# A hybrid decoder trunk: the channel sums of the convolution's layer norm move from TensorE to GpSimd, with a new order of the convolution stage

## What is computed

```python
def conv_module(xn, w_pw1, b_pw1, w_dw, b_dw, ln_g, ln_b, w_pw2, b_pw2):
    u = xn @ w_pw1 + b_pw1
    a, g = jnp.split(u, 2, axis=-1)
    u = a * jax.nn.sigmoid(g)
    u = lax.conv_general_dilated(
        u, w_dw[:, None, :].astype(u.dtype), window_strides=(1,),
        padding=[(CONV_WIDTH - 1, 0)], dimension_numbers=("NWC", "WIO", "NWC"),
        feature_group_count=u.shape[-1]) + b_dw
    u = jax.nn.silu(layer_norm(u, ln_g, ln_b))
    return u @ w_pw2 + b_pw2

h = x
for i in range(DEPTH):
    xn = rms_norm(h, g_mix[i])
    # i == 0: h = h + conv_module(...);  i == 1: h = h + nsa_attention(...)
    ...
    h = h + hier_moe(rms_norm(h, g_ffn[i]), ...)
    gate = jax.nn.sigmoid(rms_norm(h, g_ple[i]) @ ple_w_gate[i])
    h = h + gate * (p[i] @ ple_w_proj[i])
```

## Time and profile before

| | us |
|---|---|
| median of 3 runs | 1394.39 |
| lowest and highest | 1392.05 and 1396.95 |
| the profiled execution | 1397.69 |
| its span in the profile | 1395.9 |

### The profile page before, as it was taken

How to read it: one execution, slowest core, us unless ns; L and a number is a source line. 1 busy time by engine, 2 the same in 40 slices (tenths; PEclk the granted TensorE clock), 3 DMA queues, 4 the chain that set the end, 5 groups by cost and what they waited for, 6 DMA issues and landing times.

```text
span 1395.9 us, 27964 instructions
## 1 busy us (share of the span) xinstructions
PE 1070.2 (77%) x10442; PEld 602.4 (43%) x10443; DVE 310.5 (22%) x931; ACT 286.6 (21%) x664; POOL 424.4 (30%) x731
## 2 busy tenths in 40 slices
PE   6898977767767667768999889686677677676768
PEld 5673544433434334334455555343333333343433
DVE  4794310000000000004136671200000000000011
ACT  3453311111111111112112571111111111111111
POOL 2100064343343343340000130453433433452520
PEclk9998999887888888889999699898988888888979
DMA  9913379999999999994315502799999999997940
GB/s 309 389 35 132 121 304 429 428 428 429 428 428 428 428 429 428 428 424 160 127 60 211 212 30 106 317 377 428 429 428 429 429 430 428 428 428 322 430 193 31
DMA packets 62733, 448.79 MB, mean 322 GB/s; under 512 B 10826, under 2 KB 21698, under 8 KB 38114
## 3 DMA queue, kind: packets, MB, share of 16 engines
q1 hardware_dynamic: 57634, 447.73, 77.4%
q10 hardware_dynamic: 5056, 0.48, 0.3%
HBM read 447.14 MB, written 1.05 MB: 321 GB/s over the span
## 4 chain that ended last, share of the span: by engine, by line
DMA 45%; PE 42%; DVE 5%; issue 4%; ACT 2%; SPq 1%; ACTq 0%; POOL 0%; DVEq 0%
DMA ring<-in_moe_w_up 43%; PE PS L557 14%; PE PS L436 9%; PE PS L509 2%; PE PS L536 2%; DMA ring<-in_moe_w_down 2%; PE PS L572 2%; PE PS L544 1%; PE PS L763 1%; PE PS L736 1%; PE PS L579 1%; DMA ppw<-in_conv_w_dw 1%; SPq L316 1%; PE PS L819 1%; PE PS L424 1%
## 5 line engine op out<-in xcount | busy, mean ns | idle before, releaser
L557 PE MATMUL PS<-ring,arena 128*32 128x256 f32 x4128 | 342.4, 495 | 212.8 <-DMA ring<-in_moe_w_up 189.3
L557 PEld LDWEIGHTS PS<-ring,arena 128*32 128x32 f32 x4128 | 161.3, 137 | 383.3 <-issue 233.5
L1451 DVE TENSOR_TENSOR arena<-PS,arena 64x256 f32<-64x256 f32 x65 | 27.8, 428 | 637.2 <-ACT arena L1176 630.9
L572 PE MATMUL PS<-ring,arena 128*32 128x256 f32 x2080 | 125.7, 381 | 30.8 <-DVE arena L1454 30.8
L1176 ACT ACTIVATE arena<-PS 64x256 f32<-64x256 f32 x64 | 24.2, 378 | 551.1 <-PE PS L557 551.1
L977 POOL TENSOR_SCALAR arena<-arena 128x32 f32<-128x32 f32 x64 | 18.9, 295 | 342.3 <-PE PS L544 339.4
L936 POOL TENSOR_SCALAR arena<-arena 128x512 f32<-128x512 f32 x67 | 105.7, 1578 | 24.1 <-POOL arena L983 12.9
L572 PEld LDWEIGHTS PS<-ring,arena 128*32 128x32 f32 x2080 | 73.1, 109 | 61.1 <-issue 37.4
L930 POOL TENSOR_SCALAR arena<-arena 128x32 f32<-128x32 f32 x260 | 88.7, 364 | 13.1 <-POOL arena L977 12.9
L938 POOL TENSOR_TENSOR arena<-arena 128x512 f32<-128x512 f32 x67 | 85.4, 1274 | 5.6
L544 PE MATMUL PS<-hn,arena 128*32 128x256 f32 x1072 | 76.7, 401 | 9.3 <-DMA ring<-in_moe_w_down 8.9
(11 more groups left out here) (316 smaller groups left out, 1211.0 us busy)
## 6 DMA issues: line engine op xcount, KB each, us to landing
ring<-in_moe_w_up SPq DMA_DIRECT2D x64, 2048.0 KB, 22.9
ring<-in_moe_w_down SPq DMA_DIRECT2D x64, 2048.0 KB, 24.6
ring<-in_moe_w_gate SPq DMA_DIRECT2D x63, 2048.0 KB, 18.6
wb<-in_ple_w_gate SPq DMA_DIRECT2D x4, 2048.0 KB, 19.0
ring<-in_conv_w_pw SPq DMA_DIRECT2D x3, 2048.0 KB, 18.3
ring<-in_nsa_w_in SPq DMA_DIRECT2D x3, 2048.0 KB, 19.8
wb<-in_nsa_w_in SPq DMA_DIRECT2D x2, 2048.0 KB, 10.8
wb<-in_nsa_cmp_w SPq DMA_DIRECT2D x2, 2048.0 KB, 8.1
```

Source lines behind the costliest of these rows:

```text
L557: i = pe.matmul(PS[32 * j:32 * j + 32, BGU, 0:256].rearrange("q (p c) -> q p c", c=2), xT[:, k, :], w[:, k, :].rearrange("q (p h c) -> q h ...
L572: i = pe.matmul(PS[32 * j:32 * j + 32, BY, 0:Q4], hT[:, c, 32 * f:32 * f + 32], w_dn(s)[:, f, c, Q4 * j:Q4 * (j + 1)], start=(q == 0), sto ...
```

## The change

- TensorE's order becomes pw1(c), taps(c-2), and channel_sums is gone. VectorE adds the tap sum of chunk c-2 in its step c, one later than before. The pivot comes one chunk later, so chunk 2 gets it by an extra add at c = 4.
- GpSimd adds chunks 1 to 5 and their squares to lsum (layer_sums, two adds of 128x256 each); TensorE sums lsum and the chunks 6 and 7 at the end.
- The pw2 bias is loaded to all partitions (into wb's second buffer) and GpSimd adds it to the residual h in two adds of 128x1024 behind its diagonals of chunk 6. The eight one-row matmul records before taps(7) are gone. The load of the second ple_w_gate half waits for these adds, on SyncE's queue.
- The tap transposes come after pw1(0); VectorE copies wdw out after glu(0); wst is now copied from wdw by ScalarE, 16 copies between sigmoid(0) and its first stack copies.
- The small loads: the router group of layer 0 at c = 5, the router group of layer 1 and the positions behind the silus.
- mu and var use the two sigmoid buffers. VectorE's moe waits for GpSimd's bias adds.

```diff
@@ sync @@
             expert(0, 0, 0)
             sp.wait_ge(pw1_mm, 4)
-            for n in range(2):
-                sp.dma_start(dense(WB[n]), cols(ple_w_gate[0], n)).then_inc(ple_in[n], 16)
+            sp.dma_start(bpw2, conv_b_pw2.broadcast_to([P, D])).then_inc(x_in, 16)
+            sp.dma_start(dense(WB[0]), cols(ple_w_gate[0], 0)).then_inc(ple_in[0], 16)
+            sp.wait_ge(hb_ok, 2)
+            sp.dma_start(dense(WB[1]), cols(ple_w_gate[0], 1)).then_inc(ple_in[1], 16)
             sp.wait_ge(pw1_mm, 8)
-            sp.dma_start(bpw2, conv_b_pw2).then_inc(w2_in[0], 16)
             gate_up_load(0, 1, R1[0], 0, gu_in[1])
@@ tensor: taps, and the chunk loop @@
-                pe.wait_ge(xst_act, c + 1)
+                pe.wait_ge(xst_act, c + 2)
                 pe.wait_ge(xst_dve, c + 1)
...
                 i.then_inc(pw1_mm, 1)
-                if c == 2:
+                if c == 0:
+                    tap_columns()
+                if c == 3:
                     pivot_sum()
-                if c >= 1:
-                    taps(c - 1)
-                if c >= 3:
-                    channel_sums(c - 3)
-            channel_sums(KD - 3)
-            pe.wait_ge(w2_in[0], 32)
-            for n in range(2):
-                for t in range(NT):
-                    pe.matmul(PS[:, 2 * n + t, :], ones[0:1, :], bpw2[:, 512 * n:512 * (n + 1)], start=True, stop=False)
-            taps(KD - 1)
+                if c >= 2:
+                    taps(c - 2)
             for c in range(KD - 2, KD):
-                channel_sums(c)
-            pe.wait_ge(w2_in[1], 16)
+                taps(c)
+            pe.wait_ge(ln_acc, 2 * (KD - 3))
+            pe.matmul(PS[:, 6, 0:T], ones[:, :], lsum[:, 0, :], start=True, stop=False)
+            pe.matmul(PS[:, 7, 0:T], ones[:, :], lsum[:, 1, :], start=True, stop=False)
+            for c in range(KD - 2, KD):
+                pe.wait_ge(conv_ok, c + 1)
+                i = pe.matmul(PS[:, 6, 0:T], ones[:, :], cT[:, c, :], start=False, stop=(c == KD - 1))
+            i.then_inc(lnmm, 1)
+            for c in range(KD - 2, KD):
+                pe.wait_ge(ln_sq, c + 1)
+                i = pe.matmul(PS[:, 7, 0:T], ones[:, :], sqb[c % 2], start=False, stop=(c == KD - 1))
+            i.then_inc(lnmm, 1)
@@ gpsimd @@
+            def layer_sums(c):
+                if c < 3:
+                    pool.wait_ge(ln_c, c + 1)
+                else:
+                    pool.wait_ge(conv_ok, c + 1)
+                pool.wait_ge(ln_acc, 2 * (c - 1))
+                g.tensor_tensor(lsum[:, 0, :], cT[:, 0, :] if c == 1 else lsum[:, 0, :], cT[:, c, :], ALU.add).then_inc(ln_acc, 1)
+                pool.wait_ge(ln_sq, c + 1)
+                g.tensor_tensor(lsum[:, 1, :], sqb[0] if c == 1 else lsum[:, 1, :], sqb[c % 2], ALU.add).then_inc(ln_acc, 1)
+
             for c in range(KD):
                 if c >= 2:
                     pool.wait_ge(tap_mm, c - 1)
...
+                if c >= 4:
+                    layer_sums(c - 3)
+                if c == 6:
+                    pool.wait_ge(x_in, 16 * (NT + 1))
+                    pool.wait_ge(hn_dve, 1)
+                    pool.wait_ge(hn_act, 1)
+                    for t in range(NT):
+                        g.tensor_tensor(h[:, t, :], h[:, t, :], bpw2, ALU.add).then_inc(hb_ok, 1)
+            layer_sums(KD - 3)
@@ scalar @@
+                if c == 0:
+                    act.wait_ge(vec_ok, 2)
+                    for j in range(STACK):
+                        for q in range(4):
+                            i = nc.scalar.copy(wst[32 * j:32 * j + 32, q, :, :],
+                                               wdw[32 * q:32 * q + 32, :, DVE_TAPS + j::STACK])
+                    i.then_inc(xst_act, 1)
+                if c >= 3:
+                    squares(c - 3)
...
                 i.then_inc(xst_act, 1)
-                if c >= 2:
-                    squares(c - 2)
-                small_loads(c)
-            for c in range(KD - 2, KD):
+                if c == 5:
+                    router_loads(0)
+            for c in range(KD - 3, KD):
                 squares(c)
...
+            router_loads(1)
+            position_loads()
@@ vector @@
             for c in range(KD):
                 glu(c)
                 dve.wait_ge(glu_ok, c + 1)
+                if c == 0:
+                    tap_columns()
+                    dve.wait_ge(tr_ok, 4)
                 stack_copies(c)
-                if c >= 1:
-                    taps_out(c - 1)
-                if c == 0:
-                    dve.wait_ge(tr_ok, 4)
-                if c == 2:
+                if c >= 2:
+                    taps_out(c - 2)
+                if c == 4:
+                    dve.wait_ge(conv_ok, 3)
+                    v.tensor_tensor(cT[:, 2, :], cT[:, 2, :], npv, ALU.add).then_inc(ln_c, 1)
+                if c == 3:
                     dve.wait_ge(conv_ok, 2)
                     dve.wait_ge(lnmm, 1)
```

More of the change, by code:

```diff
@@ L51 @@
 XW = T + STACK * (RUNS - 1)
-N_VEC, N_MISC, N_ATT = 7, 8 + 6, 8
+N_VEC, N_MISC, N_ATT = 7, 1 + 8 + 6, 8
 SCALE = DH ** -0.5
@@ L198, in build @@
         prow = carve(512)
-        mu, var = prow[:, 0:256], prow[:, 256:512]
+        lsum = prow.rearrange("p (a t) -> p a t", a=2)
+        mu, var = sgm
         wdw = carve(8 * TAPS).rearrange("p (c w) -> p c w", c=8)
@@ L206, in build @@
         sqb = [carve(256) for _ in range(2)]
-        bpw2 = xnT[0:1, 4:8, :].rearrange("p k q -> p (k q)")
+        bpw2 = wb[:, 1, 0:D]
         wdw_rows = ppw[0:TAPS, 3072:4096]
@@ L463, in _, with tap_columns @@
             norm_T(0, 1)
-            pe.wait_ge(wdw_in, 16)
-            for c in range(KD):
-                i = pe.transpose(PS[:, 2, c * TAPS:(c + 1) * TAPS], wdw_rows[:, c * P:(c + 1) * P],
-                                 ident[0:TAPS, 0:TAPS])
-            i.then_inc(vtr, 1)
+            def tap_columns():
+                pe.wait_ge(wdw_in, 16)
+                for c in range(KD):
+                    i = pe.transpose(PS[:, 2, c * TAPS:(c + 1) * TAPS], wdw_rows[:, c * P:(c + 1) * P],
+                                     ident[0:TAPS, 0:TAPS])
+                i.then_inc(vtr, 1)
             def taps(c):
@@ L484, in pivot_sum @@
                 pe.matmul(PS[:, 6, T:2 * T], ones[:, :], cT[:, 0, :], start=True, stop=True).then_inc(lnmm, 1)
-            def channel_sums(c):
-                if c < 2:
-                    pe.wait_ge(ln_c, c + 1)
-                else:
-                    pe.wait_ge(conv_ok, c + 1)
-                i = pe.matmul(PS[:, 6, 0:T], ones[:, :], cT[:, c, :], start=(c == 0), stop=(c == KD - 1))
-                if c == KD - 1:
-                    i.then_inc(lnmm, 1)
-                pe.wait_ge(ln_sq, c + 1)
-                i = pe.matmul(PS[:, 7, 0:T], ones[:, :], sqb[c % 2], start=(c == 0), stop=(c == KD - 1))
-                i.then_inc(lnmm, 1)
             for c in range(KD):
@@ L502, in _ @@
                     pe.wait_ge(glu_ok, c - 3)
-                elif c >= 1:
-                    pe.wait_ge(vec_ok, 3)
+                elif c == 2:
+                    pe.wait_ge(vec_ok, 2)
                 for g in range(2):
@@ L536, in _ @@
                         i = pe.matmul(PS[:, 2 * n + t, :], xnT[:, k, t * P:(t + 1) * P], dense(PW2[n])[:, k, :],
-                                      start=False, stop=(k == KD - 1))
+                                      start=(k == 0), stop=(k == KD - 1))
                     i.then_inc(out_mm, 1)
@@ L758, in _ @@
             for s in range(2):
[L759 removed]
+                pe.wait_ge(w2_in[s], 32)
                 pe.wait_ge(B_ok, s + 1)
@@ L1339, in norm, with tap_columns @@
                     xnT_copy(a, row, t)
-            def first_columns():
+            def tap_columns():
                 dve.wait_ge(vtr, 2)
-                taps = PS[:, 2, 0:8 * TAPS].rearrange("p (c w) -> p c w", c=8)
-                link(v.tensor_copy(wdw, taps))
-                for j in range(STACK):
-                    for q in range(4):
-                        i = v.tensor_copy(wst[32 * j:32 * j + 32, q, :, :],
-                                          taps[32 * q:32 * q + 32, :, DVE_TAPS + j::STACK])
-                i.then_inc(vec_ok, 2)
-                dve.wait_ge(vec_ok, 3)
-                link(v.memset(cv0[:, :, 0:TAPS - 1], 0.0))
+                v.tensor_copy(wdw, PS[:, 2, 0:8 * TAPS].rearrange("p (c w) -> p c w", c=8)).then_inc(vec_ok, 1)
+                dve.wait_ge(vec_ok, 2)
             dve.wait_ge(x_in, 16 * NT)
             norm(0, ROW_MIX)
-            first_columns()
+            link(v.memset(cv0[:, :, 0:TAPS - 1], 0.0))
             def glu(c):
@@ L1396, in _ @@
                         i = v.tensor_scalar(o, u, wdw[:, c, w:w + 1], vecT[:, ROW_BDW + c:ROW_BDW + c + 1], ALU.mult, ALU.add)
-                    elif w == 1 and c < 2:
+                    elif w == 1 and c < 3:
                         i = v.tensor_scalar(o, u, wdw[:, c, w:w + 1], None, ALU.mult)
```

(11 more changed lines are left out.)

46 lines of the change are left out of this document (23 added, 23 removed).

## The result

| us | before | after |
|---|---|---|
| median of 6 runs each | 1395.67 | 1380.81 |
| lowest and highest | 1388.97 and 1400.63 | 1378.07 and 1384.35 |
| span of the profiled execution | 1395.9 | 1379.3 |

The ratio is 0.9884, with a 95% interval of 0.9859 to 0.9909: faster by 1.2%, some 15 us where 5 were forecast. Two repeats, on two chips, gave 0.9900 (0.9869 to 0.9931) and 0.9896 (0.9867 to 0.9924). The sign and the range held; the size did not. The band that the prediction thought likeliest, 1385 to 1392, was missed in all three. The range held only because it took in the time of rival B, and B's mechanism is not what happened, so that part was luck.

What follows compares the result with a forecast made beforehand. The front is bound by engines, chiefly VectorE's convolution chunks, then transfers bind the expert loops. 18.3 + 0.1 - 0.45 - 1.1 - 8.3 - 2.0 - 1.6 = 4.95 us gained, so 1394.4 - 5.0 = 1389.4 us; range 1379 to 1397.

Steps and rivals of the forecast that it cites:

- rival B: Convolution stage: GpSimd waits for gaps between VectorE's instructions, port costs 0 to 3 us, time 1381 to 1384; chance 0.24.
- What bounds the kernel: Front before the expert loads: what the convolution stage gives up moves the third expert's load and the end one for one.
- Idle time, 18.3 us: VectorE's waits before glus 3, 4, 7 and the last tap sum (6.94, 2.06, 0.41, 8.88 us) can be won.
- The start, 0.1 us: Up to glu(1): earlier pw1(0) against ScalarE's wst copies, gain about 0.1 us, bounds -1 to +1.5.
- GpSimd against VectorE, 8.3 + 1.1 us: Convolution chunks: GpSimd's new sums and bias adds block VectorE for 8.3 us (bounds 0 to 9.2), its diagonals 1.1 more.
- the signs to look for: VectorE's timeline: taps of 0.9 us and more under GpSimd's sums, and one of over 2 us at each bias add.
- Router loads, 2.0 us: Chunk 5: the first moved group holds ScalarE before sigmoid(6), making the glu late by 2.0 us, bounds 0 to 10.5.
- Tail and clock, 1.6 us: Stage end: TensorE's low clock costs 0.8 us in pw2, 0.4 on two sums, 0.4 on the last taps.
- Rival D: Pw2's first token half stays at 1.2 GHz, taking 28.1 us instead of 15.67; time 1401.0; chance 0.07.
- E: Convolution stage: VectorE still waits for glus because ScalarE is late; gain about 0, time 1394; chance 0.09.
- C: Before glu(6): ScalarE's queue held as in the first group, 10.5 us idle instead of 2; 1397.9 us; chance 0.10.
- The sum at the last tap sum: End of the convolution stage: the last tap sum would stand near 112.5 us instead of 118.6.

Runs made afterwards that it cites:

- with the loads back: The changed kernel with the small router and position loads at their old places (chunks 2, 3 and 4); 1392.9 us, ratio to before 0.9975.
- with both steps: The changed kernel with GpSimd's bias adds moved ahead of all taps and the channel sums returned to TensorE; 1378.0 us, ratio to before 0.9875.
- the kernel with the early bias: The changed kernel with the bias row loaded early and added by GpSimd ahead of all taps; 1381.1 us, ratio to before 0.9882.
- with the sums on TensorE: The changed kernel with channel sums back on TensorE, one chunk later than before, without GpSimd's ten adds; 1378.6 us, ratio to before 0.9871.

## Why the prediction was right or wrong, step by step

**What bounds the kernel: right.** The third expert's load followed the front (8.6 us earlier for 10.2 us at pw2), and the later loads by 9.8 and 9.9 us. This also held in each experiment: with the loads back, 181.0 for a last tap sum of 118.58; with both steps, 166.0 for 100.13. It is one for one from pw2 on: from there to that load it took 56.5 to 58.8 us in all twelve profiles. Between the last tap sum and pw2 a part can be lost, 5.6 us in before and 7.2 with both steps.

**Idle time, 18.3 us: right.** All of it went, but for 0.46 us in another place.

**The start, 0.1 us: mis-sized.** In the pair glu(1) moved from 35.56 to 34.09, 1.5 us, the upper bound; the other profiles of before and after (34.41 against 33.61 and 32.48) give 0.8 to 1.9. I had allowed 3.4 us for ScalarE's 16 copies and they took 4.12; but pw1(0) began right behind the first transposes:

```profile
15.16 7.51 PE L500 MATMUL PS<-xnT,wb 128*128 128x256 f32 x32
```

It took 7.51 us, while before it began at 16.98 and its gate half was ready for the sigmoid only at 26.81. So glu(0) came at 23.29 instead of 27.40, 4.1 us earlier where 2 were reckoned with; most of it is then lost to ScalarE's copies. In this profile even the first transposes of TensorE started 1.5 us later than in that of before (11.52 and 10.04). In before only 3 or 4 matmuls of pw1(0) start in each microsecond from 17 to 22, where 6 or 7 do from 22 on, and no wait for a load is recorded. They came behind an idle stretch of 2.33 us ahead of the transposes, which the new order has not. In the profile with only the loads moved the same slow stretch stands behind 1.88 us of idle time, and there the granted clock is 0.50 from 18 to 21 us. In before's own profile the clock column says 1.00, so that the clock was the cause there too is likely and not shown.

**GpSimd against VectorE, 8.3 + 1.1 us: right in the main, and by the mechanism.** Adding up what each held row of VectorE took beyond its usual time, all collisions together cost 7.95 us more than before (9.4 predicted): some 4.1 for the ten sums (5.0), 4.3 for the bias adds with the diagonal behind them (4.2). The 1.1 us more for the diagonals did not come: those that are not in the 4.3 cost 3.0 us, and in before all of them had cost 3.4. The prediction had read two of those of before as nearly whole and took two others as smaller; but the copies at 82.50 and 91.86 took 1.97 and 2.01 us too, so most of this price was already paid in before. GpSimd's rows and VectorE's:

```profile
66.60 1.24 POOL L1010 TENSOR_TENSOR arena<-stk,arena 128x512 f32<-128x512 f32 x1 [2.78 <-PE PS L481]
67.81 0.91 POOL L1002 TENSOR_TENSOR arena<-arena,hn 128x256 f32<-128x256 f32 x1
...
83.34 4.88 POOL L1019 TENSOR_TENSOR h<-h,wb 128x1024 f32<-128x1024 f32 x2
```

```profile
66.46 0.48 DVE L1425 SCALAR_TENSOR_TENSOR hn<-ppw,arena,hn 128x256 f32<-128x256 f32 x1
66.85 1.27 DVE L1425 SCALAR_TENSOR_TENSOR arena<-ppw,arena 128x256 f32<-128x256 f32 x1
68.05 0.94 DVE L1425 SCALAR_TENSOR_TENSOR hn<-ppw,arena,hn 128x256 f32<-128x256 f32 x1
```

The question that the trace of before left open is answered: a tap that starts while GpSimd works is held, 1.27 and 0.94 us instead of 0.48. The bias add took 2.44 us (4.88 for two); 2.36 had been extrapolated. Taking the sums and the bias adds away gave 7.2 us back. The bias adds fell on copies and not on taps, as the signs to look for had said, at about the same price; with the loads back they did fall on two taps, which took 2.58 and 2.56 us. Rival B is therefore wrong, though the time that it named, 1381 to 1384, is nearly the one measured: it would have had all taps at 0.48 us.

**Router loads, 2.0 us: the step that failed.** It was priced by the 4.25 us row of before, taken as the one nearest to empty queues. That row lay at 67.91, while weights were still under way; later on the same issue takes 0.46 us. The third issue of a group behind its two loads of short pieces took 12.16 and 15.22 us beside the weights, 4.25 us as they ran out, and 0.45, 0.46 and 0.46 us at 70.39, 77.76 and 78.60, when they were in. So none of the groups issued after the weights were in was held. It is not their end that frees a held issue, as the experiment with the loads back shows, and what does stays open. The weights were not in near 60 us, as had been estimated: in before they run until about 70 us, in after until about 66. The conclusion that no weights would be under way at chunk 5 was right all the same, and the estimate still took a price above nothing, so it gave back 2.0 us that were never paid.

**Tail and clock, 1.6 us: half right.** The last taps do run at the low clock, 3.64 us (granted 0.50 from 104 to 108 us), but VectorE never waited for them (0.4 predicted). Pw2 kept its time:

```profile
103.85 3.64 PE L481 MATMUL PS<-arena 128*32 128x256 f32 x32 [9.90 <-ACT arena L1139]
...
113.95 15.67 PE L533 MATMUL PS<-ring,xnT 128*128 128x512 f32 x32 [3.37 <-ACT xnT L1152]
```

The first half takes 15.67 us in both kernels; 0.8 more had been predicted. From the last tap sum to pw2 it took 6.24 us instead of 5.58, 0.7 lost for 0.4 predicted. Rival D falls with the second row, E with the missing idle time, C with the 0.46 us.

**The sum at the last tap sum.** Predicted 6.15 us earlier, measured 10.9. The difference of 4.7 us: 1.4 at the start, 2.0 for the router loads, 1.45 for GpSimd, 0.4 for the last taps, less the 0.46 of new idle time. The terms that had bounds lay inside them, but each had been set toward the same side, and four such terms add up.

**From the front to the end.** The timed runs differ by 13.7 to 14.9 us, the fronts of the first pair by 10.2 at pw2 and 9.9 later on (over the two and three profiles of the kernels, 11.1 at pw2 and 10.5 at the third expert's load). In the profiled pair 5 us more come in the attention stage, where the granted clock was low over different stretches. Windows of 10 us (busy us and records of TensorE, its weight loads, VectorE, ScalarE, GpSimd; then the clock and the DMA), before:

```profile
780.00:790.00 10.00, 5.36 (x19) 2.04 (x18) 8.14 (x33) 4.22 (x17) 2.15 (x2) 0.66 0.58 239
790.00:800.00 10.00, 9.21 (x53) 6.02 (x52) 8.86 (x46) 5.64 (x20) 2.16 (x2) 0.66 0.01 2
800.00:810.00 10.00, 10.00 (x83) 6.37 (x81) 9.82 (x52) 9.67 (x38) 4.32 (x4) 1.00 0.00 0
```

and after, some 10 us earlier:

```profile
770.00:780.00 10.00, 5.99 (x26) 4.15 (x22) 7.77 (x31) 4.20 (x17) 1.96 (x2) 0.51 0.59 246
780.00:790.00 10.00, 10.00 (x80) 6.41 (x80) 9.82 (x53) 9.38 (x38) 4.32 (x4) 0.98 0.01 2
```

Before, the clock stays at 0.66 through a second window (53 records); after, the window behind the first is already at 0.98 (80 records). From the third expert's load to the second output store it took 1203.5 to 1211.6 us over all the profiles, and 7.3 us of spread are seen between two executions of the kernel before alone. So this is a variation of executions and no gain of the change. What the timed medians have beyond the front, some 3 to 4 us, has no place of its own in the profiles. It is inside or at the edge of the intervals and stays open. The kernel with the loads back is also some 3 us below before, with a front that is equal, and the whole change is 4 us below the loads alone, with fronts that are nearly equal: both speak for something small in the rest of the change, which no run isolates.

## What to carry to other kernels

Before an elaborate reordering, look at what ended the idle times: here a queue held by the issue of a tiny load behind loads of short pieces, and moving those loads until the large ones are in is worth more than half of the change by itself (0.6% of 1.0 to 1.2%). Work given to GpSimd beside a busy VectorE was not free where both read SBUF: the length of each operation less about 0.3 us came out of VectorE, so large adds belong where VectorE waits anyway, and sums that TensorE has room for belong there. When several unknown costs are estimated, price each by the row that fits its state (queues full or empty) and keep the caution in the range, not in every term.

## What the runs showed of the hardware that was not expected

GpSimd can be held by VectorE as well, and for longer than one instruction. In the kernel after, six of the eight GpSimd operations that arrive with more than two taps of a chain begun, and with GpSimd idle ahead of them, wait to the chain's end, and then the closing add is held in turn (GpSimd, then VectorE):

```profile
39.27 3.32 POOL L1010 TENSOR_TENSOR ppw<-stk,arena 128x512 f32<-128x512 f32 x1 [5.84 <-PE PS L481]
...
57.63 4.63 POOL L1010 TENSOR_TENSOR ppw<-stk,arena 128x512 f32<-128x512 f32 x1 [5.90 <-PE PS L481]
...
80.53 2.86 POOL L1004 TENSOR_TENSOR arena<-arena 128x256 f32<-128x256 f32 x1 [3.17 <-ACT arena L1109]
```

```profile
41.79 1.08 DVE L1432 TENSOR_TENSOR hn<-hn,arena 128x256 f32<-128x256 f32 x1
...
61.46 1.08 DVE L1432 TENSOR_TENSOR hn<-hn,arena 128x256 f32<-128x256 f32 x1
```

The diagonal takes 1.05 us when nothing is in its way (72.36 in before) and 3.32 and 4.63 us here; the sum takes 0.72 and here 2.86 (behind it the next add is held to 0.77 only). The chain's taps all keep 0.48 us meanwhile, and the add that closes it takes 1.08 us instead of 0.42. The other two of the eight get in at once, or nearly, and a tap pays: the diagonal at 66.60 above, which arrives behind three instructions of its chain, and a sum behind six (GpSimd, then VectorE):

```profile
69.13 0.84 POOL L1004 TENSOR_TENSOR arena<-arena 128x256 f32<-128x256 f32 x1 [0.42 <-ACT arena L1109]
```

```profile
69.31 0.94 DVE L1425 SCALAR_TENSOR_TENSOR hn<-ppw,arena,hn 128x256 f32<-128x256 f32 x1
```

So the price to VectorE is much the same either way, one operation's length less 0.3 us, but it falls on other instructions. In the kernel with the early bias three sums get in amid a chain, behind eight, eight and thirteen instructions; one of them (GpSimd, then VectorE):

```profile
80.76 1.09 POOL L1010 TENSOR_TENSOR arena<-arena 128x256 f32<-128x256 f32 x1 [2.55 <-ACT arena L1109]
```

```profile
81.19 0.94 DVE L1425 SCALAR_TENSOR_TENSOR arena<-ppw,arena 128x256 f32<-128x256 f32 x1
```

What decides between the two stays open; the place in the chain alone does not, since with both steps a diagonal waits behind six instructions (57.31, 4.62 us) and with the sums on TensorE one gets in behind six (55.72, 1.05 us).

The Trainium skill, SBUF — State Buffer, section Who interferes with whom, says that whoever issues first gets the shared ports for the whole instruction and that the other fully blocks. The trace agrees for a single instruction on each side (1.27 us for a tap under GpSimd's diagonal of 66.60). By that rule the diagonal of 57.63 would have waited for one tap, an estimate of about half a microsecond; the trace has it take 4.63 us, 3.6 us more than when nothing is in its way, and here the measurement decides.
